# One mixing matrix for both directions of a state space stage, and the last expert tile's rows spread to tokens by TensorE

## What is computed

```python
    xdt = (x * dt[..., None])
    CB = jnp.einsum('bclgn,bcsgn->bcgls', Cc, Bc)
    Wd = CB[:, :, :, None] * segsum_exp(adt)      # exp of summed decays, lower triangle
    y_diag = jnp.einsum('bcgrls,bcsgrp->bclgrp', Wd, xdt)
...
    y_fwd = ssd_chunked(xs, dt[:, :, 0], A[0], Bm, Cm)
    y_bwd = fl(ssd_chunked(fl(xs), fl(dt[:, :, 1]), A[1], fl(Bm), fl(Cm)))
    y = y_fwd + y_bwd + d_skip.astype(f32)[:, None] * xs
```

## Time and profile before

| what | value |
|---|---|
| median of 3 runs | 2548.49 us (2546.55 to 2549.35) |
| the profiled execution's own time | 2552.66 us |
| its span, first to last instruction | 2550.4 us |
| mean granted TensorE clock | 0.94 of full |
| PE busy | 2322.0 us, 91% |
| DVE busy | 1484.2 us, 58% |
| ACT busy | 1003.9 us, 39% |
| POOL busy | 536.6 us, 21% |
| state space stage, about | 374 to 870 us of the span |
| expert stage up to the last matmul | about 2270 to 2516 us |
| from the last matmul to the end | 34 us |

### The profile page before, as it was taken

One profiled execution on the slowest core, in us unless ns is written; L12 is line 12 of the kernel. 1 busy time (PEld: TensorE's weight loads), 2 busy tenths in 40 slices (PEclk: granted clock), 3 DMA queues, 4 the chain that ended last, 5 costly groups with the idle time before them and its releaser, 6 DMA issues.

```text
span 2550.4 us, 33159 instructions
## 1 busy us (share of the span) xinstructions
PE 2322.0 (91%) x12293; PEld 1949.7 (76%) x12293; DVE 1484.2 (58%) x2225; ACT 1003.9 (39%) x1606; POOL 536.6 (21%) x613
## 2 busy tenths in 40 slices
PE   7999989999999799989999999999988997969994
PEld 6887767888888587868888878997768995757772
DVE  3555456888888754363333435567746555466664
ACT  3254523444444432353223332555333334155552
POOL 1000004555556300000000000392234440011001
PEclk8999998999999899888999999999988998979997
DMA  5310221111211433122233240322000006159995
GB/s 184 99 59 9 68 83 50 50 49 58 71 53 50 164 101 99 50 83 80 86 99 99 83 133 25 125 84 75 30 13 1 1 1 228 71 198 382 416 409 185
DMA packets 166444, 267.99 MB, mean 105 GB/s; under 512 B 9050, under 2 KB 140458, under 8 KB 156458
## 3 DMA queue, kind: packets, MB, share of 16 engines
q1 hardware_dynamic: 161849, 249.98, 28.1%
q0 software_dynamic: 4464, 16.25, 1.7%
HBM read 237.38 MB, written 28.84 MB: 104 GB/s over the span
## 4 chain that ended last, share of the span: by engine, by line
PE 68%; DVE 13%; DVEq 6%; ACT 5%; issue 4%; POOL 1%; DMA 1%; POOLq 1%; ACTq 0%; SPq 0%
PE ps L168 16%; PE ps L170 16%; PE ps L169 16%; PE ps L3410 3%; DVE arena L1631 2%; PE ps L2841 1%; PE ps L596 1%; PE ps L993 1%; ACT pair L354 1%; PE ps L2856 1%; PE ps L1015 1%; DVE arena L1667 1%; DVEq L1657 1%; DVEq L1630 1%; DVE ring_rounded L1618 1%
## 5 line engine op out<-in xcount | busy, mean ns | idle before, releaser
L170 PE MATMUL ps<-pair,pair 128*128 128x512 f32 (+1 forms) x2248 | 824.3, 367 | 0.0
L168 PE MATMUL ps<-pair,pair 128*128 128x512 f32 (+1 forms) x1992 | 750.1, 377 | 39.9 <-DVE pair L383 14.2
L169 PE MATMUL ps<-pair,pair 128*128 128x512 f32 (+1 forms) x1992 | 750.3, 377 | 0.0
L170 PEld LDWEIGHTS ps<-pair,pair 128*128 128x128 f32 x2248 | 434.3, 193 | 71.0
L168 PEld LDWEIGHTS ps<-pair,pair 128*128 128x128 f32 x1992 | 385.4, 193 | 104.5 <-issue 40.8
L169 PEld LDWEIGHTS ps<-pair,pair 128*128 128x128 f32 x1992 | 386.7, 194 | 71.0 <-issue 6.9
L354 ACT ACTIVATE pair<-ring 128x2048 fp32r<-128x2048 f32 x102 | 194.8, 1909 | 292.7 <-PE ps L170 287.0
L360 DVE TENSOR_TENSOR pair<-ring,pair 128x2048 fp32r<-128x2048 f32 x95 | 218.8, 2303 | 143.5 <-ACT pair L354 143.4
L1751 POOL TENSOR_TENSOR arena<-arena 128x256 f32<-128x256 f32 x128 | 91.4, 747 | 502.9 <-ACT arena L1528 502.9
L1743 POOL TENSOR_TENSOR pair<-arena,pair 128x512 fp32r<-128x512 f32 x128 | 156.3, 1250 | 58.2 <-PE ps L1399 58.2
L2117 POOL MEMSET arena<- 128x1 f32 x32 | 1.0, 99 | 661.4 <-DVEq L157 661.2
(11 more groups left out here) (502 smaller groups left out, 3910.1 us busy)
## 6 DMA issues: line engine op xcount, KB each, us to landing
ring<-in_w_in SPq DMA_DIRECT2D x54, 1024.0 KB, 6.5
arena<-in_w_exp_down SPq DMA_DIRECT2D x23, 1024.0 KB, 10.7
ring<-in_w_up SPq DMA_DIRECT2D x16, 1024.0 KB, 5.5
ring<-in_w_down SPq DMA_DIRECT2D x16, 1024.0 KB, 5.1
ring<-in_w_exp_gate SPq DMA_DIRECT2D x16, 1024.0 KB, 8.8
ring<-in_w_exp_up SPq DMA_DIRECT2D x16, 1024.0 KB, 10.8
expert_results<-arena SPq DMA_DIRECT2D x23, 512.0 KB, 11.2
ring<-in_w_in SPq DMA_DIRECT2D x16, 512.0 KB, 5.7
```

The costliest lines, as they stand in the source:

```text
L168: nc.tensor.matmul(out, lhs[1], rhs[0], start=start, stop=False)
L169: nc.tensor.matmul(out, lhs[0], rhs[1], start=False, stop=False)
L170: return nc.tensor.matmul(out, lhs[0], rhs[0], start=False, stop=stop)
```

## The change

In the state space stage the two mixing matrices of a chunk become one. The sums of both directions are accumulated in one PSUM bank (off the diagonal of a chunk one of the two is zero), there is one exponential per chunk, and the result is multiplied by `cb_forward * dt_forward + cb_backward * dt_backward`, which ACT and DVE build per head. The product within the chunk takes the plain tokens `xt` and one matrix, so half of its matmuls go, and so do POOL's two `weighted` calls with `dt`. The matrices of all four chunks have a buffer each.

In the expert stage the last tile's result isn't stored to DRAM. It stays in SBUF, and PE spreads its rows to tokens with a matrix of shares (made by POOL from `of_slot`, turned by PE, copied by ACT). The same PSUM group takes the second gathered row times a diagonal matrix of shares. DVE adds the first gathered row and the PSUM result. Tokens that had a row in the last tile gather another tile's row with share zero. The last tiles' order on PE, ACT and DVE is changed, and so is the order of the tail on DVE.

```diff
-                def sums(g, n):
...
+                def sums(g, c):
+                    if c == 0:
                         pe.wait_ge(z_stored, g * 4 + 4)
+                    if c >= 2:
+                        pe.wait_ge(ex_ready, g * 4 + (c - 1))
+                    for d, mask in enumerate((strict.hi, strict.lo)):
+                        pe.wait_ge(am_ready, g * 8 + (2 * c + d + 1))
+                        nc.tensor.matmul(ps[:, SUMS[c % 2], :], mask[:, 0, :], am[d].lo[:, 0, :], start=d == 0, stop=False)
+                        mm = nc.tensor.matmul(ps[:, SUMS[c % 2], :], mask[:, 0, :], am[d].hi[:, 0, :], start=False, stop=d == 1)
+                    mm.then_inc(diff_ready, 1)
...
                         for r in range(GH):
-                            for d in range(2):
-                                mm = nc.tensor.matmul(ps[:, 7, r * 64:(r + 1) * 64],
-                                                      M[:, (2 * c + d) % 4, r * P:(r + 1) * P],
-                                                      xw[:, d, c, r * 64:(r + 1) * 64], start=d == 0, stop=d == 1)
+                            mm = nc.tensor.matmul(ps[:, 7, r * 64:(r + 1) * 64], M[:, c, r * P:(r + 1) * P],
+                                                  xt[:, c, r * 64:(r + 1) * 64], start=True, stop=True)
...
+                def forward_steps(g, c):
+                    act.wait_ge(cb_read, g + 1)
+                    for r in range(GH):
+                        ins = act.activation(stepped[:, c, r * P:(r + 1) * P], cb[:, 0, c, :], ACT.Copy,
+                                             scale=step_of(g, 0, c, r))
+                    ins.then_inc(forward_stepped, 1)
...
                         if c + 1 < NT:
-                            decay(g, 2 * c + 2)
-                            decay(g, 2 * c + 3)
+                            forward_steps(g, c + 1)
+                            decay(g, c + 1)
...
-                def mixers(g, n):
...
+                def mixers(g, c):
+                    dve.wait_ge(forward_stepped, g * 4 + (c + 1))
+                    for r in range(GH):
+                        both = stepped[:, c, r * P:(r + 1) * P]
+                        dve.scalar_tensor_tensor(out=both, in0=cb[:, 1, c, :], scalar=step_of(g, 1, c, r), in1=both,
+                                                 op0=ALU.mult, op1=ALU.add)
+                    dve.drain()
+                    dve.wait_ge(ex_ready, g * 4 + (c + 1))
+                    dve.tensor_tensor(M[:, c, :], ex[:, c % 2, :], stepped[:, c, :], ALU.mult).then_inc(m_ready, 1)
...
                 def steps(g, n):
                     c, d = n // 2, n % 2
-                    if n >= 2:
-                        gp.wait_ge(diff_ready, g * 8 + (n - 1))
+                    if c and d == 0:
+                        gp.wait_ge(diff_ready, g * 4 + c)
...
-                    weighted(g, 2, wst)
-                    weighted(g, 3, wst)
-                    for n in range(2):
-                        steps(g, n)
-                    weighted(g, 0, dt)
-                    weighted(g, 1, dt)
-                    for n in range(2, 4):
+                    weighted(g, 0, wst)
+                    weighted(g, 1, wst)
+                    for n in range(4):
                         steps(g, n)
...
+                def join_rows():
+                    pe.wait_ge(*exps.at(2))
+                    pe.wait_ge(*y_act.at(TILES))
+                    pe.wait_ge(*y_dve.at(TILES))
+                    for t in range(NT):
+                        for half in range(2):
+                            nc.tensor.matmul(ps[:, JOIN_BANKS[t][half], :], last_turned[:, t, :],
+                                             y[LAST % 2][:, half * 512:(half + 1) * 512], start=True, stop=False)
+                        pe.wait_ge(s_back[t], 32)
+                        for half in range(2):
+                            mm = nc.tensor.matmul(ps[:, JOIN_BANKS[t][half], :], second_diag[:, t, :],
+                                                  back[:, 1, t, half * 512:(half + 1) * 512], start=False, stop=True)
+                        mm.then_inc(down_made.sem, 1)
...
+                up(LAST, range(0, 4))
+                turn_act(LAST - 1)
+                up(LAST, range(4, 6))
+                down(LAST - 1)
+                up(LAST, range(6, DC))
+                turn_act(LAST)
+                down(LAST)
+                join_rows()
...
                 def join(t):
                     dve.wait_ge(s_back[t], 32)
...
+                    dve.scalar_tensor_tensor(out=x_tok[:, t, :], in0=back[:, 0, t, :], scalar=share[:, 0, t:t + 1],
+                                             in1=x_tok[:, t, :], op0=ALU.mult, op1=ALU.add)
+                    dve.drain()
+                    dve.wait_ge(*down_made.at(TILES + t + 1))
+                    for half in range(2):
+                        part = x_tok[:, t, half * 512:(half + 1) * 512]
+                        ins = dve.tensor_tensor(part, ps[:, JOIN_BANKS[t][half], :], part, ALU.add)
...
+                scaled(0)
                 join(3)
+                scaled(1)
                 variance(2)
+                roots(2)
+                scaled(2)
+                scaled(3)
...
+                def last_tile(i):
+                    if i == 4:
+                        gp.tensor_tensor(last_share, in_tile[:, :, LAST], flat_share, ALU.mult)
+                        gp.drain()
+                        gp.tensor_tensor(of_slot, of_slot, last_share.unsqueeze(2).to_broadcast([P, 2 * NT, P]), ALU.mult)
+                    if i == 6:
+                        gp.drain()
+                        gp.tensor_tensor(flat_share, flat_share, last_share, ALU.subtract)
+                        gp.tensor_tensor(last_parts, of_slot[:, 0:NT, :], of_slot[:, NT:2 * NT, :], ALU.add)
...
-                gp.wait_ge(s_y[0], 16 * (TILES - TILES // 2))
-                gp.wait_ge(s_y[1], 16 * (TILES // 2))
+                gp.wait_ge(*up_made.at(TILES))
+                gp.wait_ge(s_y[0], 16 * (LAST - LAST // 2))
+                gp.wait_ge(s_y[1], 16 * (LAST // 2))
```

More of the change, by code:

```diff
@@ L1264, in stages_ssd @@
             Bt = core.take(NT, D_STATE)
-            xw = core.take(4, NT, GW)
+            xw = core.take(2, NT, GW)
+            stepped = core.take(NT, GH * P)
             xd = core.take(NT, GW)
@@ L1370, in ssd_sync, with step_of @@
                     load_z(g + 1)
+            def step_of(g, d, c, r):
+                return dt[:, d, c, columns(g * GH + r, 1)]
             def ssd_tensor(pe):
@@ L1438, in front @@
                     turn_last()
[L1440 removed]
+                    pe.wait_ge(xw_ready, g * 2 + 2)
                     pe.wait_ge(tok_ready, g * 3 + 3)
@@ L1449, in front @@
                     sums(g, 0)
-                    sums(g, 1)
+                    after(pe, y_stored, g * 2)
                 def back(g, between):
@@ L3258, in stages_moe @@
             y = [small[:, (6 + 4 * i) * DE:(10 + 4 * i) * DE] for i in range(2)]
+            last_parts, last_turned, second_diag = (h_tok[:, 2 + i // 2, i % 2 * 512:(i % 2 + 1) * 512]
+                                                    .rearrange("p (t n) -> p t n", t=NT) for i in range(3))
+            last_share = h_tok[:, 3, 512:512 + 2 * NT]
+            LAST = TILES - 1
+            JOIN_BANKS = ((0, 1), (2, 3), (5, 6), (4, 7))
             core.top = mark
@@ L3692, in join @@
                     dve.wait_ge(s_back[t], 32)
-                    for n in range(2):
-                        dve.drain()
-                        ins = dve.scalar_tensor_tensor(out=x_tok[:, t, :], in0=back[:, n, t, :], scalar=share[:, n, t:t + 1],
-                                                       in1=x_tok[:, t, :], op0=ALU.mult, op1=ALU.add)
+                    dve.scalar_tensor_tensor(out=x_tok[:, t, :], in0=back[:, 0, t, :], scalar=share[:, 0, t:t + 1],
+                                             in1=x_tok[:, t, :], op0=ALU.mult, op1=ALU.add)
+                    dve.drain()
+                    dve.wait_ge(*down_made.at(TILES + t + 1))
+                    for half in range(2):
+                        part = x_tok[:, t, half * 512:(half + 1) * 512]
+                        ins = dve.tensor_tensor(part, ps[:, JOIN_BANKS[t][half], :], part, ALU.add)
                     ins.then_inc(joined.sem, 1)
@@ L3702, in variance, with roots, scaled @@
                         .then_inc(var_made.sem, 1)
-                def last_norm(t):
+                def roots(t):
                     dve.wait_ge(*root_made.at(t // 2 + 1))
                     newton_rsqrt(core, dve, *(z[:, t:t + 2] for z in (var, root, newton)))
-                    if t == 0:
-                        dve.wait_ge(s_router[0], 64 + 16)
-                    for n in (t, t + 1):
-                        dve.scalar_tensor_tensor(out=x_tok[:, n, :], in0=x_tok[:, n, :], scalar=root[:, n:n + 1], in1=gain,
```

(13 more changed lines are left out.)

125 lines of the change are left out of this document (63 added, 62 removed).

## The result

The changed kernel takes 2581.30 us in the median of 4 runs (2580.31 to 2583.80), the kernel before beside it 2548.92 (2546.55 to 2549.66). The ratio is 1.014, with a 95% interval of 1.0124 to 1.0155 (the two medians alone give 1.013). The forecast was 2529.8 with a range up to 2543; the change makes the kernel slower.

The account below looks back on a forecast made before the run. It took DVE to bind the state space stage beside PE. Stage -13.6, experts +0.5 and tail -5.6 us sum to -18.7, so the median 2548.49 becomes 2529.8 us; range 2514 to 2543.

Parts of the forecast that it names:

- What the small operations cost under POOL's steps no row shows: State space stage, DVE: all eight small operations of the first two chunks taken to cost 0.2 us more beside POOL.
- a quarter of 0.85: State space stage, DVE: upper end for small operations beside POOL, 0.2 us more each, or 1.7 us for eight.
- DVE's mixers: State space stage: building the mixing matrices on DVE takes 1.1 us more per middle group (0.2 + 0.45 + 0.45).
- 0.45 us more: State space stage, DVE: extra time per chunk after the first two, 1.7 us against 1.2 to 1.3.
- Waits of the mixers: State space stage: DVE's 11.1 us of waits for the exponential before the third chunk's matrices shrink by 7.5 us.
- The sum of the stage: State space stage: 7 x (1.1 - 1.7) - 7.5 - 1.9 = -13.6 us.
- POOL's gift to DVE: State space stage: without POOL's multiplications DVE gains 1.3 us in scaling y and 0.4 in weight splits, 1.7 per group.
- PE's halves: State space stage: 16 matmul records per chunk become 8, about 32 us in eight groups, not taken since DVE binds.
- Tail: End of the kernel: gathers start 7.2 us earlier; -7.3 us at full clock, -5.6 after 1.7 us for slow clock.
- the rival with the low clock in the tail: End of the kernel: PE stays at 1.2 GHz through joining rows, ending 3 us later than before, 2539; chance 0.1.
- slower by the mixers: State space stage: small operations at full cost plus gaps, 5.5 us more per group than taken, total 2576; chance 0.05.
- The two-input rule holds: State space stage: DVE operations with two SBUF inputs stretch beside POOL, 1.7 us per group, total 2541.7; chance 0.15.

Follow-up runs that it names:

- light_pool_early: Changed kernel with POOL's steps of groups 1 to 7 writing one head of four and ACT's copies for chunks 1 to 3 moved earlier: 2514.4 us.
- tail_only: Kernel before with only the experts' and the tail's part of the change: 2539.32 us against 2545.93, a ratio of 0.9972.

## Why the prediction was wrong

**The step that failed** is the sentence "What the small operations cost under POOL's steps no row shows", and the term built on it: 0.2 us for all eight small operations of the first two chunks, where the changed kernel has 2.8 us for the four of chunk 0 alone (3.95 less 1.13). A row does show the price, in the trace of the kernel before. DVE's and POOL's timelines of the kernel before, the root of a middle group:

```profile
587.20 0.18 DVE L681 RECIPROCAL arena<-arena 128x4 f32<-128x4 f32 x1 [1.02 <-ACT arena L1560]
587.46 0.29 DVE L683 TENSOR_TENSOR arena<-arena 128x4 f32<-128x4 f32 x1
587.82 0.92 DVE L685 TENSOR_TENSOR arena<-arena 128x4 f32<-128x4 f32 x1
588.83 0.92 DVE L687 TENSOR_SCALAR arena<-arena 128x4 f32<-128x4 f32 x1
589.83 0.92 DVE L689 TENSOR_TENSOR arena<-arena 128x4 f32<-128x4 f32 x1
```

```profile
586.69 4.03 POOL L1743 TENSOR_TENSOR pair<-arena,pair 128x512 fp32r<-128x512 f32 x4
```

Three operations of four columns, at a pitch of 1 us, exactly while POOL's steps run. (L683 began late in a step and takes 0.29 us, until about that step's end.) In the last group, where POOL is idle by then, the same lines take 0.16 us. Even the upper end, "a quarter of 0.85", scaled the price by the width, on which it hardly depends. By these rows four small operations under POOL's steps cost about 4 us, as they do. The row that I leaned on, L1631, was no witness: of its 128 operations only one meets POOL's steps L1743, and that one (674.58 us) had begun 0.4 us before them. Those above 0.8 us lie beside POOL's multiplications L1751, which stretch it by little.

**DVE's mixers.** Predicted 1.1 us more per group. In the group shown they take 7.21 + 3.53 + 1.90 = 12.6 us (548.57 to 555.78, 566.46 to 569.99, 577.64 to 579.54) against 5.09 + 2.58 + 1.28 = 8.95: 3.7 more. The group stands for the others: over the stage the lines' busy time goes from 72.4 us (L1667) to 99.2 (71.6 of L1674 and 27.6 of L1678), 26.8 more in eight groups. The uncontended part was sized nearly right: 1.13 us for four against 0.9, and 1.90 for a whole chunk against 1.7. A second error hid in "0.45 us more" for chunk 2: it starts from the 1.28 us of a free pair, while the earlier trace rows show 2.58 for chunk 2, beside POOL's steps. Chunk 2 went from 2.58 to 3.53 us.

**Waits of the mixers.** Predicted to shrink by 7.5 us, to 3.6. They grew to 19.4. The prediction counted the copies' time on ACT (0.2 us each, 0.8 for four; four take 1.26) and not their place: for chunks 1 to 3 they stand behind the copy of u and the weight split. This is 16 us apart; by light_pool_early the waits cost nothing once POOL's steps are light.

**The sum of the stage.** -13.6 us predicted, +31.8 measured, 45 us apart. With the group shown for all seven, the mixers are 7 x (3.7 - 1.1) = 18 us of it, and the waits 16. The other 11 us I can't divide by rows. In them are PE's clock in the stage, down from 0.95 to 0.91 (windows, 420 to 820 us), PE's 22.9 us of waits for weight splits, which were 1.0 us before, and the carries L1663, 3.97 us in a group (1.61 + 2.36) against 3.74 of L1655, beside POOL's steps in both.

**POOL's gift to DVE** was right: the scaling of y 1.14 us for four in a middle group, 1.3 less, and the two splits 2.36 us against 2.88, 0.5 less, where 1.7 together was taken. **PE's halves** were right too: 1.00 us at full clock for 1.89. POOL's gift is in DVE's time and counts; PE's halves give nothing back once PE waits for DVE.

**Tail.** -5.6 us predicted (-5.1 with the experts' new work), -6.6 measured by tail_only. The copy of the result of the last tile but two, in the kernel before and in the changed one:

```profile
2501.58 0.69 DVE L3687 COPY arena<-ps 128x512 f32<-128x512 f32 x1 [1.58 <-PE ps L3410]
```

```profile
2536.07 0.69 DVE L3739 COPY arena<-ps 128x512 f32<-128x512 f32 x1 [1.59 <-PE ps L3422]
```

The first gather of the changed kernel, and PE's part:

```profile
2548.24 0.94 POOL L3825 DMA_INDIRECT arena<-expert_results,arena  x1 [34.51 <-DMA expert_results<-arena]
```

```profile
2551.71 1.96 PE L3439 MATMUL ps<-arena 128*128 128x512 f32 x4 [0.88 <-DVE arena L3739]
2554.63 1.98 PE L3443 MATMUL ps<-arena 128*128 128x512 f32 x4 [0.96 <-DMA arena<-expert_results,arena]
2556.45 1.88 PE L3439 MATMUL ps<-arena 128*128 128x512 f32 x4
```

This copy starts 34.5 us later than before, and the first gather starts only 28.3 us later than the 2519.91 of the earlier trace rows: 6.2 us won, 7.2 predicted. From there to the end it is 30.4 us, and was 30.5. Two waits of 0.9 us didn't bring the clock down: it is 1.00 from 2520 to 2560. So the rival with the low clock in the tail is out, and so are the 1.7 us that the sum took for the clock. The tail's total came out within 1 to 2 us because the gathers gained 1 us less and the clock cost 1.7 us less; the mechanism was right, the closeness is partly luck.

**The rivals.** The one that came true had the lowest chance, 0.05: slower by the mixers, 2576. Its size came out near the 2581 by luck, and its mechanism is half right: it had the mixers 6.6 us longer per group with the waits as before, and they are 3.7 longer with 8 us more of waits. It took 0.2 us for each small operation beside POOL and made up the rest with operations that don't overlap; they do overlap (1.13 us for four), and the price is 0.7 us each. "The two-input rule holds" named the mechanism, but it priced it by columns at 1.7 us per group, where the small operations alone pay (3.95 - 1.13) + (2.77 - 1.13) = 4.5. With the four-column rows read, 2.8 us more in chunk 0 alone would have been above the 2.7 us per group from which, by the prediction's own sum, the change is slower.

## What to carry to other kernels

Before cutting a VectorE operation into small ones beside a busy GpSimd, look in the trace for VectorE's smallest operations in the same stretch. If four columns cost as much as GpSimd's instruction lasts, count one such wait for each instruction. Fewer and wider operations save waits, shorter GpSimd instructions shorten them, and an operand in PSUM took the one form tried here out of them; each has to be weighed against what it does to the other engines' waits. And work that is moved to a third engine is priced by its place in that engine's order, not by its duration.

## What the runs showed of the hardware

- A VectorE operation beside GpSimd's 128x512 product of 1.08 us takes about 1.0 to 1.1 us at 128x128 (0.35 where GpSimd is idle) and 0.92 at 128x4 (0.16); beside halves of about 0.6 us, 0.7 to 0.8 and 0.49.
- A tensor_tensor of 128x512 with one operand in PSUM isn't stretched: at most 0.692 us in 64, against 1.52 in the median with both in SBUF.
- RECIPROCAL L681 (0.18 us) isn't stretched in the same stretch; TENSOR_SCALAR L687, with one tensor from SBUF, is. No run takes apart which forms wait. Beside GpSimd's 128x256 products (L1758) a scalar_tensor_tensor of 128x512 (L1639) mostly takes 0.85 us in place of 0.75, once 1.15, while four scalings of 128x256 (L1706) take 2.48 us in place of 1.14 beside L1751; why isn't settled either.
- Light GpSimd steps gave the kernel before 36 us of stage: contention cost it more than the busy time of L1667 shows, since TensorE's waits go (14.1 to 2.5 us for L1471) and its clock in the stage rises from 0.95 to 0.99.
